# Two decoder layers in one kernel: a new order of the VectorE and ScalarE work in the MLPs' down projections

## Chip, core and metric

The kernel runs on one core of one Trainium2 chip. The metric is the device time of one execution in microseconds (us), as the median of several runs; a lower time is better.

## What is computed

The reference is two layers of a decoder trunk over 1024 tokens and a model width of 1024. Each layer has a mixer (sparse attention with a gated recurrence in layer 0, a gated recurrence with windowed attention in layer 1), an output projection, and a squared-ReLU MLP with 4096 hidden units. The change touches the two MLPs alone:

```python
for layer in range(DEPTH):
    h = rms_norm(x, norm_mix_g[layer])
    ...
    x = x + mix
    h = rms_norm(x, norm_mlp_g[layer])
    x = x + jnp.square(jax.nn.relu(h @ mlp_w_up[layer])) @ mlp_w_down[layer]
```

## The kernel before

Every float32 matrix product is made of three matmuls. An operand is split in a rounded high part (`w_hi`, `uo_hi`, `h_hi`) and the rest (`w_lo`, `uo_lo`, `h_lo`), and the products high by high, low by high and high by low are added up in PSUM. ScalarE makes the high parts, by a copy that rounds. The low part of a weight is a subtraction on GpSimd (`low`, line 936, POOL in the profile), the low part of an activation one on VectorE (`low`, line 2592, DVE).

An MLP runs over eight groups of 512 hidden units. The first is done directly. The others, and the down projection of the first seven, go by a scheme that takes seven products of half-size blocks in place of eight, at the price of sums and differences of the operands. A middle group (`group(i)`, i from 1 to 6) has on TensorE seven up products P0 to P6 and seven down products e0 to e6, each of 24 matmuls of 512 columns. The first group has, behind its up part, a short stretch of matmuls that forms sums of `h` (`combinations`), and then its own e0 to e6. The last group has P0 to P6 and then a plain down projection by four weight units (`down_last`).

The activations of a group are four quarters `quarter(r, c)`. The down products read seven operands made from them: e0 reads quarter (1,1); e1 the difference `s3` (`uo_sum`); e2 the difference `ub` = (1,1) - s3; e3 quarter (0,0); e4 quarter (0,1); e5 quarter (1,0) after (1,1) has been added to it (line 2629); e6 the difference of (0,1) and `ub` (line 2612). Three pairs of buffers `uo_hi`, `uo_lo` hold the operands in turn (`S_OPERAND`), so that the operand of e3 can be written once e1 has been done, that of e4 once e0 has, and so on. TensorE waits ahead of e0 to e6 for 1, 2, 3, 5, 5, 6 and 7 low parts (`LOW_COUNT`) and for one more weight each time.

The down weights of a group are three sums `d1`, `d0`, `d2`, made on GpSimd (line 943) out of four raw blocks, and the four raw blocks. The products of e0 to e6 are left in four pairs of PSUM banks in turn (`S_BANKS`), and VectorE adds them to `x` and `shared` (line 2609). A product may only begin when VectorE has read the pair of banks that it takes.

All engines run their own instructions in the order in which they are written, with semaphores between them. Nothing reorders: a wait holds all that is written behind it. On ScalarE a group ends with `late_operands`, which copies the operands of e3 to e6 and the last two down weights; the first weight of the next group (`UP_SLOTS[0]`) stands behind it. GpSimd's next group begins with the low part of that weight. The raw blocks are loaded by SyncE, each as soon as GpSimd has used the one before in its buffer.

## Time and profile before

| | |
|---|---|
| median of 3 runs | 2649.71 us (2647.24 to 2653.09) |
| profiled execution, own time | 2644.74 us |
| its span | 2643.0 us |
| TensorE (PE) busy | 2380.4 us, 90% |
| GpSimd (POOL) busy | 1422.0 us, 54% |
| VectorE (DVE) busy | 1763.9 us, 67% |
| ScalarE (ACT) busy | 1142.0 us, 43% |

The span is that of one profiled execution. A row of the timeline gives start and duration of one or more instructions of a kind in a row on one engine, and in brackets how long the engine was idle before and what released it. The MLP of layer 0 lies at about 780 to 1520 us, that of layer 1 at about 1905 to the end.

### The profile page before, as it was taken

To read this page: it belongs to the slowest core of one execution; us is meant where nothing else is said; L and a number is where in the kernel's file an instruction comes from. 1 tells how busy PE (TensorE), PEld (TensorE's weight loads), DVE (VectorE), ACT (ScalarE), POOL (GpSimd) and SP (SyncE) were. 2 spreads that over 40 slices of the span, in tenths; PEclk is the share of its full clock that TensorE was granted. 3 is DMA by queue.
4 is the path that set the end of the run, shared out by engine and by line. 5 is a ranking of instruction groups with operands and counts; after the bars stand their busy time and mean duration, and the time that the engine had idled before them with its cause. 6 is when DMAs were issued, how large, how long until landed. Compare 5 with 4: busy or idle time off the path is not lost.

```text
span 2643.0 us, 31005 instructions
## 1 busy us (share of the span) xinstructions
PE 2380.4 (90%) x10811; PEld 1916.8 (73%) x10833; DVE 1763.9 (67%) x2390; ACT 1142.0 (43%) x1867; POOL 1422.0 (54%) x719
## 2 busy tenths in 40 slices
PE   8899997889899988898889999889998888988998
PEld 6678874558887766686668777767876667766777
DVE  7879879889854576457647557666555764575473
ACT  4556887676554233323332455354532333233320
POOL 3203427998724665766577222255145657565762
PEclk9999998999999999999999999989999999999999
DMA  5311130022013432433244222221034233423342
GB/s 158 90 38 51 49 100 5 17 59 78 9 49 127 144 118 75 148 135 110 80 150 133 84 84 56 72 78 32 24 143 144 82 109 135 146 84 111 133 137 80
DMA packets 167356, 241.57 MB, mean 91 GB/s; under 512 B 27529, under 2 KB 110546, under 8 KB 167250
## 3 DMA queue, kind: packets, MB, share of 16 engines
q1 hardware_dynamic: 160786, 233.65, 27.2%
q10 hardware_dynamic: 6464, 6.56, 0.8%
q8 instruction: 60, 0.98, 0.2%
q14 instruction: 46, 0.38, 0.0%
HBM read 204.25 MB, written 26.21 MB: 87 GB/s over the span
## 4 chain that ended last, share of the span: by engine, by line
PE 28%; POOL 26%; issue 23%; DVE 11%; ACT 6%; DMA 5%; SPq 1%; POOLq 0%; ACTq 0%; another core or an unknown queue 0%; DVEq 0%
POOL w_lo L936 13%; PE ps L2805 7%; PE ps L2806 7%; PE ps L2807 7%; DMA w_raw<-in_mlp_w_down 4%; POOL w_sum L943 4%; POOL w_raw L943 3%; ACT signs L1669 3%; POOL PL L1146 2%; POOL cl L1188 1%; POOL w_lo L923 1%; PE ps L2798 1%; POOL w_hi L917 1%; DVE ps L2363 1%; DVE ps L2261 1%
## 5 line engine op out<-in xcount | busy, mean ns | idle before, releaser
L936 POOL TENSOR_TENSOR w_lo<-w_raw,w_hi 128x1024 fp32r<-128x1024 f32 x148 | 384.6, 2615 | 346.5 <-ACT w_hi L1478 309.3
L2805 PE MATMUL ps<-w_hi,uo_hi 128*128 128x512 f32 x784 | 320.5, 409 | 145.4 <-DVE uo_lo L2592 140.2
L923 POOL TENSOR_TENSOR w_lo<-w_raw,w_hi 128x1024 fp32r<-128x1024 f32 x61 | 159.4, 2613 | 353.4 <-ACT w_hi L1692 349.6
L2806 PE MATMUL ps<-w_lo,uo_hi 128*128 128x512 f32 x784 | 315.5, 402 | 0.0
L2807 PE MATMUL ps<-w_hi,uo_lo 128*128 128x512 f32 x784 | 315.0, 402 | 0.0
L2805 PE MATMUL ps<-h_hi,w_hi 128*128 128x512 f32 x776 | 311.5, 401 | 0.0
L2807 PE MATMUL ps<-h_hi,w_lo 128*128 128x512 f32 x776 | 303.8, 392 | 0.0
L2806 PE MATMUL ps<-h_lo,w_hi 128*128 128x512 f32 x776 | 303.6, 391 | 0.0
L2609 DVE TENSOR_TENSOR x_res<-ps,x_res 128x1024 f32<-128x1024 f32 x224 | 265.1, 1216 | 46.5 <-PE ps L2807 40.3
L2805 PEld LDWEIGHTS ps<-w_hi,uo_hi 128*128 128x128 f32 x784 | 154.4, 197 | 190.1 <-issue 152.4
L1478 ACT ACTIVATE w_hi<-w_raw 128x1024 fp32r<-128x1024 f32 x143 | 148.9, 1053 | 252.6 <-PE ps L2807 188.4
L2807 PEld LDWEIGHTS ps<-w_hi,uo_lo 128*128 128x128 f32 x784 | 153.4, 196 | 33.7
L2806 PEld LDWEIGHTS ps<-w_lo,uo_hi 128*128 128x128 f32 x784 | 154.5, 197 | 31.6
L2979 PE MATMUL ps<-h_hi,w_hi 128*128 128x512 f32 x448 | 174.3, 389 | 0.0
L2980 PE MATMUL ps<-h_lo,w_hi 128*128 128x512 f32 x448 | 174.3, 389 | 0.0
L2981 PE MATMUL ps<-h_hi,w_lo 128*128 128x512 f32 x448 | 174.3, 389 | 0.0
L2807 PEld LDWEIGHTS ps<-h_hi,w_lo 128*128 128x128 f32 x776 | 146.3, 189 | 31.6
L2806 PEld LDWEIGHTS ps<-h_lo,w_hi 128*128 128x128 f32 x776 | 146.6, 189 | 30.0 <-issue 1.9
L2805 PEld LDWEIGHTS ps<-h_hi,w_hi 128*128 128x128 f32 x776 | 146.4, 189 | 30.4 <-issue 2.4
L936 POOL TENSOR_TENSOR w_lo<-w_sum,w_hi 128x1024 fp32r<-128x1024 f32 x56 | 156.5, 2815 | 11.6 <-ACT w_hi L1478 7.6
L2673 DVE TENSOR_TENSOR ps<-ps,ub 128x1024 f32<-128x1024 f32 x14 | 17.3, 1233 | 203.9 <-ACT ps L1590 203.9
L1478 ACT ACTIVATE w_hi<-w_sum 128x1024 fp32r<-128x1024 f32 x56 | 57.9, 1058 | 201.2 <-POOL w_sum L943 201.2
(436 smaller groups left out, 5882.5 us busy)
## 6 DMA issues: line engine op xcount, KB each, us to landing
uo_hi<-scr_h SPq DMA_DIRECT2D x82, 512.0 KB, 3.9
uo_lo<-scr_h SPq DMA_DIRECT2D x82, 512.0 KB, 4.8
w_raw<-in_mlp_w_up SPq DMA_DIRECT2D x64, 512.0 KB, 3.6
w_raw<-in_mlp_w_down SPq DMA_DIRECT2D x64, 512.0 KB, 5.2
w_raw<-in_even_w_in SPq DMA_DIRECT2D x23, 512.0 KB, 3.9
x_res<-in_x SPq DMA_DIRECT2D x16, 512.0 KB, 7.8
t<-xg SPq DMA_DIRECT2D x120, 64.0 KB, 2.0
scr_h<-h_hi SPq DMA_DIRECT2D x12, 512.0 KB, 7.6
```

What stands on the lines that cost most here:

```text
L923: g.tensor_tensor(w_lo[:, k, :], w_raw[:, n % 2, :], w_hi[:, k, :].bitcast(F32), ALU.subtract).then_inc(w_ready, 1)
L936: g.tensor_tensor(w_lo[:, slot, :], source, w_hi[:, slot, :].bitcast(F32), ALU.subtract) \
L943: g.tensor_tensor(out_, in0, in1, op).then_inc(sums_ready, 1)
L1478: s.activation(w_hi[:, slot, :], source, ACT.Copy).then_inc(w_hi_ready, 1)
L1669: s.activation(signs[:, 0:w], keys, ACT.Sign, bias=tkc[:, q - 2:q - 1], accum_out=cnt[:, q - 2:q - 1]).then_inc(level_counted, 1)
L2609: ins = v.tensor_tensor(dst, ps[:, bank:bank + 2, :], dst, ALU.add)
L2805: t_.matmul(out_, ah, bh, start=first, stop=False)
L2806: t_.matmul(out_, ah, bl, start=False, stop=False)
L2807: return t_.matmul(out_, al, bh, start=False, stop=last)
L2979: t_.matmul(out_, ah, bh, start=begins and k == 0, stop=False, skip_group_check=not begins)
L2980: t_.matmul(out_, ah, bl, start=False, stop=False, skip_group_check=not begins)
L2981: ins = t_.matmul(out_, al, bh, start=False, stop=k == 3, skip_group_check=not begins)
```

## The change

VectorE in a middle group: the sum that completes quarter (1,0) (`mixed`) goes from ahead of the down products' additions to behind those of e2. The rest of `s3` goes ahead of the squaring of quarter (0,1). The difference for e6 (`last_sum`) and the low parts for e3 to e6 get new places among the additions (`downs`). The first group keeps its old order under the name `first_downs`.

ScalarE in a middle group: operand e0 is copied ahead of the weight sum for e0; the relu of quarter (1,0) goes ahead of the other two weight sums; two raw weights go behind the copies for e1 and e2. In `late_operands` the copies for e3 and e4 and the last two weights change places, and the copy for e5 now waits for `mixed`.

TensorE in the first group waits for the sums of `h` bank by bank and no longer for all of them. In the last group ScalarE rounds the four last weight units (`last_unit`), which GpSimd did before (`split_high`); two of these units take other slots (`LAST_SLOTS`).

```diff
-        LAST_SLOTS = (2, 3, 4, 5)
+        LAST_SLOTS = (2, 5, 3, 4)
...
                 for n in range(n0 + MLP_UNITS - 4, n0 + MLP_UNITS):
-                    split_unit(n)
+                    split_low(n)
...
                 def late_operands(i, slots):
 
+                    sums_at(i, 0)
+                    operand(4, quarter(0, 1))
                     act.wait_ge(raw_landed[2], 32 * i + (l0[2] + 32))
-                    sums_at(i, 0)
+                    if slots is not FIRST_SLOTS:
+                        weights(slots[5], raws[2])
+                    sums_at(i, 1)
+                    operand(3, quarter(0, 0))
                     if slots is FIRST_SLOTS:
                         sums_at(i, 2)
-                    weights(slots[5], raws[2])
-                    operand(4, quarter(0, 1))
+                        weights(slots[5], raws[2])
                     act.wait_ge(raw_landed[3], 32 * i + (l0[3] + 32))
-                    sums_at(i, 1)
                     weights(slots[6], raws[3])
-                    operand(3, quarter(0, 0))
+                    act.wait_ge(u_squared, 4 * i + (q0 + 3))
                     sums_at(i, 2)
                     operand(5, quarter(1, 0))
                     act.wait_ge(u_squared, 4 * i + (q0 + 4))
...
+                def last_unit(j):
+                    n = n0 + MLP_UNITS - 4 + j
+                    act.wait_ge(raw_landed[n % 2], landed[n])
+                    for used in last_uses(n):
+                        act.wait_ge(*used)
+                    s.activation(w_hi[:, slot_of(n), :], w_raw[:, n % 2, :], ACT.Copy).then_inc(w_hi_ready, 1)
...
+                    add_sums(i, 0, 0)
+                    add_sums(i, 0, 2)
+                    add_sums(i, 1, 0)
+                    low(i, 4, 4, quarter(0, 1))
+                    low(i, 5, 3, quarter(0, 0))
+                    add_sums(i, 1, 2)
+                    add_sums(i, 2, 0)
+                    add_sums(i, 2, 2)
+                    mixed()
+                    last_sum()
+                    add_sums(i, 3, 0)
+                    low(i, 6, 5, quarter(1, 0))
+                    add_sums(i, 3, 2)
+                    summed(i, 4)
+                    low(i, 7, 6, ub[:])
+                    for e in range(4, 7):
+                        add_sums(i, e, 0)
+                        add_sums(i, e, 2)
...
+                            if slots is FIRST_SLOTS and d in (0, 3) and t % 2 == 0:
+                                pe.wait_ge(quarters_done, first_rests(layer) + (14 if d == 0 else 16))
...
-                    pe.wait_ge(quarters_done, first_rests(layer) + 16)
```

The first place is VectorE's order in a middle group, from the squaring of quarter (1,0) to e0's additions. Before:

```order
1001 L2662 TENSOR_TENSOR u_all<-ps,u_all 128x2x512
1003 L2625 TENSOR_TENSOR uo_sum<-u_all 128x1024
1006 L2662 TENSOR_TENSOR u_all<-ps,u_all 128x2x512
1007 L2628 TENSOR_TENSOR ub<-u_all,uo_sum 128x1024
1008 L2629 TENSOR_TENSOR u_all<-u_all 128x2x512
1011 L2592 TENSOR_TENSOR uo_lo_64<-uo_sum,uo_hi_61 128x1024
1013 L2592 TENSOR_TENSOR uo_lo_65<-ub,uo_hi_62 128x1024
1016 L2609 TENSOR_TENSOR x_res<-ps,x_res 128x2x512
```

And now:

```order
1001 L2705 TENSOR_TENSOR u_all<-ps,u_all 128x2x512
1003 L2670 TENSOR_TENSOR uo_sum<-u_all 128x1024
1005 L2672 TENSOR_TENSOR ub<-u_all,uo_sum 128x1024
1008 L2608 TENSOR_TENSOR uo_lo_64<-uo_sum,uo_hi_61 128x1024
1010 L2705 TENSOR_TENSOR u_all<-ps,u_all 128x2x512
1012 L2608 TENSOR_TENSOR uo_lo_65<-ub,uo_hi_62 128x1024
1015 L2624 TENSOR_TENSOR x_res<-ps,x_res 128x2x512
```

`uo_lo_64` is the low part for e1. It stood behind a squaring (line 2662), `ub` and the sum of quarter (1,0); now only `ub` stands between it and `s3`.

The second place is VectorE among the additions of the down products, now, where `uo_lo_63`, `uo_lo_64` and `uo_lo_65` are the low parts for e4, e3 and e5:

```order
1019 L2624 TENSOR_TENSOR x_res<-ps,x_res 128x2x512 x2
1021 L2608 TENSOR_TENSOR uo_lo_63<-u_all,uo_hi_60 128x1024
1023 L2608 TENSOR_TENSOR uo_lo_64<-u_all,uo_hi_61 128x1024
1025 L2624 TENSOR_TENSOR x_res<-ps,x_res 128x2x512 x2
1027 L2624 TENSOR_TENSOR shared<-ps,shared 128x1024
1029 L2624 TENSOR_TENSOR shared<-ps,shared 128x1024
1030 L2631 TENSOR_TENSOR u_all<-u_all 128x2x512
1031 L2628 TENSOR_TENSOR ub<-u_all,ub 128x1024
1033 L2624 TENSOR_TENSOR shared<-ps,shared 128x1024
1034 L2624 TENSOR_TENSOR x_res<-ps,x_res 128x2x512
1036 L2608 TENSOR_TENSOR uo_lo_65<-u_all,uo_hi_62 128x1024
```

The sum of quarter (1,0) and the difference for e6 now stand in the middle of the additions, ahead of those of e3.

The third place is ScalarE in a middle group, from the relu of quarter (0,0) on. Before:

```order
731 L1566 ACTIVATE u_all<-ps 128x2x512
733 L1478 ACTIVATE w_hi<-w_sum 128x1024
735 L1481 ACTIVATE uo_hi_60<-u_all 128x1024
737 L1478 ACTIVATE w_hi<-w_sum 128x1024 x2
739 L1566 ACTIVATE u_all<-ps 128x2x512
741 L1478 ACTIVATE w_hi<-w_raw 128x1024
743 L1481 ACTIVATE uo_hi_61<-uo_sum 128x1024
```

And now:

```order
731 L1576 ACTIVATE u_all<-ps 128x2x512
733 L1481 ACTIVATE uo_hi_60<-u_all 128x1024
735 L1478 ACTIVATE w_hi<-w_sum 128x1024
737 L1576 ACTIVATE u_all<-ps 128x2x512
739 L1478 ACTIVATE w_hi<-w_sum 128x1024 x2
741 L1481 ACTIVATE uo_hi_61<-uo_sum 128x1024
```

The relu of quarter (1,0) (the second `u_all<-ps`) now comes ahead of the two weight copies, and e0's operand ahead of the first of the three.

## Rows read from the trace of the kernel before

**Rows 1.** The page, head and part 1.

```profile
span 2643.0 us, 31005 instructions
...
PE 2380.4 (90%) x10811; PEld 1916.8 (73%) x10833; DVE 1763.9 (67%) x2390; ACT 1142.0 (43%) x1867; POOL 1422.0 (54%) x719
```

**Rows 2.** Waits of PE: who, for whom, us in all, times, longest.

```profile
PE ps L2805 <- DVE uo_lo L2592: 140.2, 14, 10.4
```

**Rows 3.** Timeline of PE, layer 0: first matmuls behind the MLP's long waits.

```profile
838.16 0.50 PE L2805 MATMUL ps<-w_hi,uo_hi 128*128 128x512 f32 x1 [1.66 <-DVE h_lo L2649]
...
865.23 0.77 PE L2805 MATMUL ps<-w_hi,uo_hi 128*128 128x512 f32 x1 [10.45 <-DVE uo_lo L2592]
...
942.45 0.79 PE L2805 MATMUL ps<-w_hi,uo_hi 128*128 128x512 f32 x1 [9.94 <-DVE uo_lo L2592]
...
1119.59 0.79 PE L2805 MATMUL ps<-w_hi,uo_hi 128*128 128x512 f32 x1 [9.94 <-DVE uo_lo L2592]
...
1386.01 0.79 PE L2805 MATMUL ps<-w_hi,uo_hi 128*128 128x512 f32 x1 [9.96 <-DVE uo_lo L2592]
...
1462.75 0.80 PE L2805 MATMUL ps<-w_hi,u_hi 128*128 128x512 f32 x1 [3.65 <-POOL w_lo L923]
```

**Rows 4.** Timeline of PE around the start of one group's e0.

```profile
1103.33 0.39 PE L2979 MATMUL ps<-h_hi,w_hi 128*128 128x512 f32 x1
...
1104.01 0.40 PE L2805 MATMUL ps<-w_hi,uo_hi 128*128 128x512 f32 x1
```

**Rows 5.** Stretches: us, busy us of PE, PEld, DVE, ACT, POOL, PE's clock, DMA.

```profile
1463.00:1468.00 5.00, 5.00 (x12) 3.88 (x13) 2.63 (x1) 0.00 (x0) 4.92 (x3) 0.50 0.36 105
838.10:840.10 2.00, 1.94 (x8) 1.61 (x9) 0.00 (x1) 0.93 (x1) 1.94 (x1) 1.00 0.00 0
```

**Rows 6.** Timeline of DVE ahead of e1 in one middle group.

```profile
1100.15 1.38 DVE L2592 TENSOR_TENSOR uo_lo<-u_all,uo_hi 128x1024 fp32r<-128x1024 f32 x1 [4.33 <-ACT uo_hi L1481]
...
1104.69 2.54 DVE L2625 TENSOR_TENSOR uo_sum<-u_all 128x1024 f32<-128x1024 f32 x1
...
1112.81 3.37 DVE L2629 TENSOR_TENSOR u_all<-u_all 128x1024 f32<-128x1024 f32 x1
1116.30 3.15 DVE L2592 TENSOR_TENSOR uo_lo<-uo_sum,uo_hi 128x1024 fp32r<-128x1024 f32 x1
1119.38 1.21 DVE L2592 TENSOR_TENSOR uo_lo<-ub,uo_hi 128x1024 fp32r<-128x1024 f32 x1
```

**Rows 7.** Timeline of POOL in the same stretch.

```profile
1098.03 2.42 POOL L943 TENSOR_TENSOR w_sum<-w_sum,w_raw 128x1024 f32<-128x1024 f32 x1
1100.60 8.90 POOL L936 TENSOR_TENSOR w_lo<-w_sum,w_hi 128x1024 fp32r<-128x1024 f32 x3 [0.16 <-POOL w_sum L943]
1109.45 8.92 POOL L936 TENSOR_TENSOR w_lo<-w_raw,w_hi 128x1024 fp32r<-128x1024 f32 x3
```

**Rows 8.** Timeline of ACT in the same stretch: the relu of quarter (1,0).

```profile
1102.39 1.01 ACT L1566 ACTIVATE u_all<-ps 128x1024 f32<-128x1024 f32 x1
```

**Rows 9.** Timelines of ACT, POOL and DVE around the end of e3.

```profile
1049.80 1.06 ACT L1481 ACTIVATE uo_hi<-ub 128x1024 fp32r<-128x1024 f32 x1 [4.38 <-PE ps L2807]
...
1051.88 2.39 POOL L936 TENSOR_TENSOR w_lo<-w_raw,w_hi 128x1024 fp32r<-128x1024 f32 x1 [9.42 <-ACT w_hi L1478]
...
1052.07 3.28 DVE L2592 TENSOR_TENSOR uo_lo<-ub,uo_hi 128x1024 fp32r<-128x1024 f32 x1
```

**Rows 10.** Timeline of DVE: four additions of down products in a row.

```profile
1036.65 4.62 DVE L2609 TENSOR_TENSOR x_res<-ps,x_res 128x1024 f32<-128x1024 f32 x4
```

**Rows 11.** Timeline of POOL between the up and the down weights.

```profile
1083.41 2.41 POOL L943 TENSOR_TENSOR w_raw<-w_raw,w_raw 128x1024 f32<-128x1024 f32 x1 [6.34 <-DMA w_raw<-in_mlp_w_down]
```

**Rows 12.** Timeline of ACT in the first group, behind e2.

```profile
854.90 1.06 ACT L1478 ACTIVATE w_hi<-w_raw 128x1024 fp32r<-128x1024 f32 x1 [15.88 <-PE ps L2807]
```

**Rows 13.** Timeline of POOL ahead of the last down projection: rounding, then rest.

```profile
1457.51 1.90 POOL L917 TENSOR_TENSOR w_hi<-w_raw,onec 128x1024 fp32r<-128x1024 f32 x1
1459.49 3.21 POOL L923 TENSOR_TENSOR w_lo<-w_raw,w_hi 128x1024 fp32r<-128x1024 f32 x1
```

More of the change, by code:

```diff
@@ L2622, in operands, with add_sums @@
-                def operands(i, n):
-                    if n == 0:
-                        v.tensor_tensor(s3, quarter(0, 0), quarter(1, 0), ALU.subtract).then_inc(u_squared, 1)
-                        summed(i, 1)
-                    if n == 1:
-                        v.tensor_tensor(ub[:], quarter(1, 1), s3, ALU.subtract).then_inc(u_squared, 1)
-                        v.tensor_tensor(quarter(1, 0), quarter(1, 0), quarter(1, 1), ALU.add).then_inc(u_squared, 1)
-                        summed(i, 3)
+                def add_sums(i, e, t):
+                    k = S_ORDER[e]
+                    dve.wait_ge(down_done, S_SUMS * i + (g0 + 4 * e + t + 2))
+                    earlier = [n for n in range(e) if set(S_TARGETS[S_ORDER[n]]) & set(S_TARGETS[k])]
+                    if earlier:
+                        dve.wait_ge(x_added, S_SUMS * i + (g0 + 4 * earlier[-1] + t + 2))
+                    for c in S_TARGETS[k]:
+                        dst = shared[:, t:t + 2, :] if c is None else                             x[:, 4 * (1 - c[0]) + t:4 * (1 - c[0]) + t + 2, c[1] * HT:(c[1] + 1) * HT]
+                        bank = S_BANKS[2 * e + t // 2]
+                        ins = v.tensor_tensor(dst, ps[:, bank:bank + 2, :], dst, ALU.add)
+                    ins.then_inc(x_added, 2)
@@ new lines, in last_sum, with mixed, first_downs @@
+                def last_sum():
+                    v.tensor_tensor(ub[:], quarter(0, 1), ub[:], ALU.subtract).then_inc(u_squared, 1)
+                def mixed():
+                    v.tensor_tensor(quarter(1, 0), quarter(1, 0), quarter(1, 1), ALU.add).then_inc(u_squared, 1)
+                def first_downs():
+                    for e in range(7):
+                        add_sums(0, e, 0)
+                        add_sums(0, e, 2)
+                        if e == 0:
+                            last_sum()
+                            low(0, 4, 4, quarter(0, 1))
+                        if e == 1:
+                            low(0, 5, 3, quarter(0, 0))
+                        if e == 2:
+                            low(0, 6, 5, quarter(1, 0))
+                        if e == 3:
+                            summed(0, 4)
+                            low(0, 7, 6, ub[:])
@@ L2632, in first_group, with operands @@
+                def operands(i):
+                    v.tensor_tensor(s3, quarter(0, 0), quarter(1, 0), ALU.subtract).then_inc(u_squared, 1)
+                    summed(i, 1)
+                    v.tensor_tensor(ub[:], quarter(1, 1), s3, ALU.subtract).then_inc(u_squared, 1)
+                    summed(i, 2)
                 def first_group():
@@ L2641, in first_group @@
                             dve.wait_ge(proj_free, h0 + 6)
-                            operands(0, 0)
-                            operands(0, 1)
+                            operands(0)
+                            mixed()
                             low(0, 2, 1, s3)
@@ L2686, in group @@
                         dve.wait_ge(quarters_done, quarters + C12_DONE)
-                        operands(i, 0)
+                        operands(i)
+                        low(i, 2, 1, s3)
                     last_low(3, 1, 0)
@@ L2692, in group @@
                         return
-                    operands(i, 1)
-                    low(i, 2, 1, s3)
                     low(i, 3, 2, ub[:])
```

48 lines of the change are left out of this document (17 added, 31 removed).

## The prediction, made before the run

> **What bounds the kernel now.** The page says that TensorE is busy for 90% of the span and VectorE for 67% [rows 1]. A busy share says nothing of single waits, so the waits of TensorE come next: one line alone makes 140.2 us of them in 14 waits, and it waits for a low part of VectorE [rows 2]. The timeline of TensorE shows where: in each MLP once in the first group (10.45 us) and once in each of six middle groups (9.94 us, each ahead of e1) [rows 3]. The period from one such wait to the next is (1386.01 - 942.45) / 5 = 88.7 us.
>
> A wait costs more than its length. Three matmuls take 1104.01 - 1103.33 = 0.68 us at full clock [rows 4], 0.227 us each and 5.44 us for a product of 24. Behind the wait of 3.65 us, 12 matmuls fill 5.0 us at a granted clock of 0.50, which is the lower level of 1.2 GHz; behind the wait of 1.66 us the clock stays at 1.00 [rows 3, 5]. The middle group has 14 products, 76.2 us. Of the 88.7 us, 12.5 are left: 9.94 us of wait, about 2.3 us of halved clock, and 0.2 us of small change.
>
> What does VectorE do before e1? Four operations between SBUF operands stand in line: `s3`, `ub`, the sum of quarter (1,0), the low part for e1. The first, third and fourth take 2.54, 3.37 and 3.15 us, while the next one of the same kind, with GpSimd idle, takes 1.21 [rows 6]. GpSimd's low parts take 2.4 us alone, but three of them take 8.90 and again 8.92 us [rows 7]. Laid side by side, each starts when the other ends: VectorE's sum of 1104.69 ends at 1107.23, one operation behind the end of GpSimd's second low part. I read it as: these operations take turns, 2.4 us for GpSimd, 1.2 for VectorE. The Trainium skill (SBUF — State Buffer, SBUF: two separate sides) says that the two engines share a pair of ports as an exclusive lock, which whoever starts first holds for the whole instruction, VectorE only with two SBUF inputs. The durations agree. Were they merely long and GpSimd not held, the delays of GpSimd below would drop out, and the sum would be that of the first rival.
>
> **The change, part by part.** I count from E, the end of a group's e3; in the group shown it is 1049.65 (ScalarE is released at 1049.80 [rows 9]). From there TensorE has e4 to e6 and P0 to P6, ten products, 54.4 us, and e0 does start at 1104.01 [rows 4]. GpSimd's chain to the weight for e0 also begins at E, with the first weight of the next group at E + 2.2 [rows 9]; it contains a 6.3 us wait for blocks from memory [rows 11], and its low part for e0 ends about 3.2 us behind 1100.60, at E + 54.1 [rows 7]. So today e0 starts with hardly 0.3 us in hand. Whatever slows GpSimd's chain stops e0.
>
> *Ahead of e0.* e0's operand no longer stands behind a weight that waited for GpSimd. VectorE is idle for 4.33 us before that operand's low part at 1100.15 [rows 6], so quarter (1,1) was done at 1095.8; with a copy of 1.06 us the low part can be asked for at 1097.0. It then falls ahead of GpSimd's sum `d0`, which began at 1098.03 [rows 7], and pushes it back by 1.15 us, to an end at 1101.6. The relu of quarter (1,0) began at 1102.39 [rows 8]; its product P5 ends 5.44 us before e0 starts, at 1098.6, and only one weight copy is now ahead of it, so it begins at 1099.1. With 1.0 us for it and 1.2 for the squaring `s3` is asked for at 1101.4, just before `d0` ends. If it takes its turn there, GpSimd's low part for e0 ends 1.2 us later than today, and e0 starts at E + 55.5 in place of 54.4. TensorE loses 1.2 us.
>
> *Ahead of e1.* `s3` ends at E + 53, GpSimd's low part for e0 at 55.3, `ub` at 56.5, the next low part at 58.8, and the low part for e1 at 59.9. e1 is wanted at 55.5 + 5.4 = 60.9. The wait of 9.94 us and its 2.3 us of low clock go. The squaring of quarter (0,1) and the low part for e2 end within 2.5 us of e1's start; e1's second half and e2 need them after 2.7 and 5.4.
>
> *Among the additions*, from T, e1's start. An addition costs 4.62 / 4 = 1.15 us [rows 10]. Low part for e2 to T + 2.5, four additions to 7.0, low part for e4 to 8.3, then GpSimd's turn to 10.7, low part for e3 to 11.8. e3 is wanted at T + 10.9, so it waits about 1.05 us; E is T + 17.4. VectorE ends the additions of e2 at T + 16.3, `mixed` at 17.5 and the difference for e6 at 18.6. ScalarE, which stood free at E, now waits for `mixed` with the copy for e5, and behind it are queued the copy for e6 and the first weight of the next group; GpSimd waits for that. It begins at E + 3.4 in place of 2.2. The low part for e5 meets it, which it did not before, and the one for e6 also does, as before (3.28 us [rows 9]). GpSimd is 2.4 us late in all. The wait of 6.3 us for memory [rows 11] gives back between none and all of that, as the blocks asked for later have fewer transfers ahead; I take 0.8, nearer to none, because an unhindered load cannot land before it is asked for. VectorE is late too, and e6's second half waits 1.5 us for the bank that e5's additions free; if GpSimd had its turn before the low part for e5, e5 waits 1.65 and e6 2.2 us.
>
> *Sum of a middle group that follows a middle group.* GpSimd's chain is 54.1 + 1.6 (late start and meetings, less the memory's gift), and 1.2 to 2.4 more ahead of e0, where the turns fall worse once it is late: e0 at about E + 57.3, e1 at E + 62.8; if `s3` loses its turn, E + 64.4. With 17.4 the period is 80.2 to 81.8. I take 81.0, so 7.7 us saved, five times in each MLP: 38.5.
>
> *The first group.* TensorE starts its e0 when 14 of 16 sums are read, 1.2 us sooner. ScalarE's copies for e4 and e3 stood behind a weight that waited for the end of e2 (15.88 us idle, then released by TensorE [rows 12]); they now follow e0 and e1. Counted from the start of e0, VectorE comes behind its end (5.6) to one addition, the difference for e6, e4's low part, four additions and e3's low part: 5.6 + 1.15 + 1.2 + 1.2 + 4.6 + 1.2 = 15.0. e2 ends at 16.3. So the 10.45 us wait goes, with 1.6 us of low clock: 13.3 us. Its order on VectorE is the old one, so the next group only loses the 1.2 us at e0: its wait of 9.94 and 0.2 less 1.2 makes 9.2.
>
> *The last group.* From T of group 6 to the last down projection it is 1462.75 - 1386.01 = 76.7 us; now 17.4 + 1.5 + 54.4 + 0.5 = 73.8, 2.9 less. ScalarE's rounding takes four operations of 1.9 us off GpSimd, whose last low part ended at 1462.70 [rows 13]; the four come behind each other's loads, and the last is then ready at about the end of P6, 1459. What is left (0.5) is the low part for the third quarter. Without the 3.65 us wait the clock does not fall: 5.0 us [rows 5] for 12 matmuls in place of 2.7, and a few more, 2.6 us. Together 5.5. Bounds: nothing is gained if the weights are as late as now (0), 6.3 if all goes.
>
> *Moved at no cost:* two raw weights on ScalarE come 4 us later, but GpSimd takes them only when its three other low parts are done; the slots are mere places.
>
> Sum for an MLP 13.3 + 9.2 + 38.5 + 5.5 = 66.5, for both 133 us. The profiled execution took 2644.7 us, which gives 2512; it lies 5.0 us (0.2%) below the median of 2649.7, which gives 2517. I say 2515.
>
> **The rivals.**
> *All is hidden (17%).* VectorE's and GpSimd's turns fall well, or VectorE is early enough. With no stall left, 14 waits of 12.4 us, twice 1.2 and twice 6.3 give 189 us, 2461; with 2.2 us left in each period 161, 2489. For it: GpSimd has idle stretches of nearly 10 us [rows 9]. Against: they lie ahead of its chain, and in the chain there is 0.3 us in hand.
> *Short waits drop the clock (27%).* My waits of 1.4 to 2.9 us lie between 1.66 us, which left the clock at 1.00, and 3.65, which halved it [rows 3, 5]. One drop in each of twelve groups costs 12 x 2.4 = 29 us (2545), two 58 (2573). The Trainium skill (TensorE: Matmul & The Clock Gate, Part 1) says that the clock is halved by how busy the array has been and not by single waits, and that the moment varies; by it some of these would be charged.
> *ScalarE's new wait makes it slower (2%).* Each us by which `mixed` ends behind E delays everything on GpSimd by one. It decides against the change from 11 us on, with `mixed` at E + 12: some 10 additions late. Twelve groups at 13 us late would give 2660. VectorE would have to lose three times what I count.
> *No change (2%).* GpSimd's chain grows until the period is 88.7 again. It would need 7.7 us more meetings, six per group; I count two or three new ones.
>
> **How the numbers follow.** My case, 2490 to 2535, has 50%; all hidden 17, clock 27, neither 2 and 2, and 2 for more than 2590. The range 2476 to 2562 leaves out part of the first rival and the two-drop end of the second. A measurement here tells 0.2% (5 us) from nothing: faster by more 0.96, within 0.02, slower 0.02.
>
> **What would show it.** In the waits of TensorE the 140.2 us line should fall below 30 us in 14 or more short waits; e1's wait should be gone. Waits for GpSimd's weight ahead of e0 should be 1 to 3 us, for VectorE's low part ahead of e3 about 1 us, for additions ahead of e6's second half 1 to 2 us. The period should be 80 to 82 us. The first weight of a group should start on GpSimd 3.4 us behind E. I am wrong if e1 still waits over 2 us, or if the clock is halved in most groups.

## The result and the profile after

The changed kernel takes 2511.16 us (median of 4 runs, 2503.55 to 2514.51), the kernel before, timed beside it, 2649.45 us. The ratio is 0.9473 [0.9448, 0.9498], 138 us less; the forecast was 2515 us. The profiled execution took 2513.01 us, 131.7 less than that of before; by this pair, on which the sum was made, the forecast was 133.

The page of the changed kernel, head and part 1 (against [rows 1]):

```profile
span 2510.3 us, 31037 instructions
...
PE 2362.6 (94%) x10833; PEld 1901.0 (76%) x10833; DVE 1742.0 (69%) x2390; ACT 1151.5 (46%) x1875; POOL 1444.4 (58%) x711
```

The engines do the same work, but for eight roundings of weights that went from GpSimd to ScalarE. VectorE is busy for 22 us less, as fewer of its operations stretch beside GpSimd. GpSimd is busy for 22 us more in spite of the eight: more of its own now stretch beside VectorE. TensorE is busy for 18 us less, as fewer matmuls run at half clock. The waits of TensorE (who, for whom, us in all, times, longest), the rows of the MLPs (against [rows 2]):

```profile
PE ps L2847 <- POOL w_lo L936: 14.6, 12, 1.8
...
PE ps L2847 <- DVE x_res L2624: 9.8, 10, 1.0
...
PE ps L3022 <- DMA uo_lo<-scr_h: 7.1, 9, 1.7
PE ps L2847 <- DVE uo_lo L2608: 6.4, 12, 2.0
```

One line of 140.2 us in 14 waits has become four kinds of short waits, 37.9 us in 43. The third kind is for a streamed piece: a part of the split `h` that SyncE loads back from memory (`scr_h`) during a group, for the up products. The timeline of TensorE shows where the waits stand (against [rows 3]): e0 of the first group and of three middle groups, the other waits of the one at 1159.11 (e3, e6's second half), the longest e1, and the last down projection of layer 0.

```profile
839.16 0.47 PE L2847 MATMUL ps<-w_hi,uo_hi 128*128 128x512 f32 x1 [0.55 <-DVE h_lo L2692]
...
1004.74 0.49 PE L2847 MATMUL ps<-w_hi,uo_hi 128*128 128x512 f32 x1 [2.05 <-DVE uo_lo L2608]
...
1078.39 0.49 PE L2847 MATMUL ps<-w_hi,uo_hi 128*128 128x512 f32 x1 [0.99 <-POOL w_lo L936]
...
1159.11 0.49 PE L2847 MATMUL ps<-w_hi,uo_hi 128*128 128x512 f32 x1 [1.65 <-POOL w_lo L936]
...
1175.96 0.49 PE L2847 MATMUL ps<-w_hi,uo_hi 128*128 128x512 f32 x1 [0.24 <-DVE uo_lo L2608]
...
1196.27 0.50 PE L2847 MATMUL ps<-w_hi,uo_hi 128*128 128x512 f32 x1 [0.99 <-DVE x_res L2624]
...
1239.89 0.49 PE L2847 MATMUL ps<-w_hi,uo_hi 128*128 128x512 f32 x1 [1.79 <-POOL w_lo L936]
...
1402.16 0.77 PE L2847 MATMUL ps<-w_hi,u_hi 128*128 128x512 f32 x1 [2.76 <-issue]
```

From one e0 to the next it is 1159.11 - 1078.39 = 80.7 and 1239.89 - 1159.11 = 80.8 us. In the group at 1159 nothing waits ahead of e1. In two of the twelve middle groups e1 still waits, 2.05 us at 1004.74 and 2.01 us at 1987.54. The stretch from the first e0 to the last down projection was 1462.75 - 838.16 = 624.6 us in layer 0 and is 563.0 now; in layer 1 it went from 626.7 to 561.6.

VectorE from `ub` on in that group (against [rows 6]; the row at 1171.22 holds the low parts for e4 and e3, the one at 1180.28 is `mixed`):

```profile
1156.79 3.28 DVE L2672 TENSOR_TENSOR ub<-u_all,uo_sum 128x1024 f32<-128x1024 f32 x1
1160.19 3.24 DVE L2608 TENSOR_TENSOR uo_lo<-uo_sum,uo_hi 128x1024 fp32r<-128x1024 f32 x1
...
1171.22 4.61 DVE L2608 TENSOR_TENSOR uo_lo<-u_all,uo_hi 128x1024 fp32r<-128x1024 f32 x2
...
1180.28 1.21 DVE L2631 TENSOR_TENSOR u_all<-u_all 128x1024 f32<-128x1024 f32 x1
```

`s3` took 1.22 us there, at 1155.53, just ahead of GpSimd's low part for e0 (1155.75). In the group whose e1 waits at 1004.74 GpSimd's came first, and `s3` ends a turn later; VectorE's and GpSimd's timelines:

```profile
995.22 2.71 DVE L2670 TENSOR_TENSOR uo_sum<-u_all 128x1024 f32<-128x1024 f32 x1
```

```profile
994.44 9.09 POOL L936 TENSOR_TENSOR w_lo<-w_sum,w_hi 128x1024 fp32r<-128x1024 f32 x3 [0.16 <-POOL w_sum L943]
```

ScalarE and GpSimd behind the end of e3, which is 1175.96 + 5.44 = 1181.4 (against [rows 9]): operand e5 comes behind `mixed`, then e6's, then the first weight, and GpSimd takes it at 1184.8.

```profile
1181.60 1.06 ACT L1481 ACTIVATE uo_hi<-u_all 128x1024 fp32r<-128x1024 f32 x1 [9.27 <-DVE u_all L2631]
1182.73 1.06 ACT L1481 ACTIVATE uo_hi<-ub 128x1024 fp32r<-128x1024 f32 x1
1183.70 1.04 ACT L1478 ACTIVATE w_hi<-w_raw 128x1024 fp32r<-128x1024 f32 x1
```

```profile
1184.82 3.46 POOL L936 TENSOR_TENSOR w_lo<-w_raw,w_hi 128x1024 fp32r<-128x1024 f32 x1 [6.72 <-ACT w_hi L1478]
```

### The profile page after: what moved, and what is told of

Same layout as the page of the kernel before. It is cut to its first block, busy times and chain, and to the rows that moved or that the text cites. A ratio compares the mean times of both kernels' runs of the same rounds, so it can differ in the third digit from the quotient of the medians.

```text
span 2510.3 us, 31037 instructions
## 1 busy us (share of the span) xinstructions
PE 2362.6 (94%) x10833; PEld 1901.0 (76%) x10833; DVE 1742.0 (69%) x2390; ACT 1151.5 (46%) x1875; POOL 1444.4 (58%) x711
## 4 chain that ended last, share of the span: by engine, by line
PE 34%; POOL 22%; issue 17%; DVE 13%; DMA 6%; ACT 6%; SPq 1%; POOLq 0%; ACTq 0%; DVEq 0%
POOL w_lo L936 11%; PE ps L2847 8%; PE ps L2849 8%; PE ps L2848 8%; DMA w_raw<-in_mlp_w_down 5%; POOL w_sum L943 4%; ACT signs L1685 3%; POOL w_raw L943 2%; POOL PL L1146 2%; POOL cl L1188 1%; PE ps L2840 1%; PE ps L3022 1%; PE ps L3024 1%; PE ps L3023 1%; DVE ps L2379 1%
## 5 line engine op out<-in xcount | busy, mean ns | idle before, releaser
L936 POOL TENSOR_TENSOR w_lo<-w_raw,w_hi 128x1024 fp32r<-128x1024 f32 x148 | 407.9, 2775 | 169.9 <-ACT w_hi L1478 132.6
L923 POOL TENSOR_TENSOR w_lo<-w_raw,w_hi 128x1024 fp32r<-128x1024 f32 x61 | 154.4, 2533 | 368.5 <-ACT w_hi L1708 349.9
L2847 PE MATMUL ps<-w_hi,uo_hi 128*128 128x512 f32 x784 | 310.8, 396 | 31.9 <-POOL w_lo L936 14.6
L2848 PE MATMUL ps<-w_lo,uo_hi 128*128 128x512 f32 x784 | 306.9, 391 | 0.0
L2849 PE MATMUL ps<-w_hi,uo_lo 128*128 128x512 f32 x784 | 306.9, 391 | 0.0
L2847 PEld LDWEIGHTS ps<-w_hi,uo_hi 128*128 128x128 f32 x784 | 147.9, 189 | 77.2 <-issue 33.0
L1481 ACT ACTIVATE uo_hi<-u_all 128x1024 fp32r<-128x1024 f32 x56 | 59.5, 1062 | 282.9 <-DVE u_all L2631 105.4
L936 POOL TENSOR_TENSOR w_lo<-w_sum,w_hi 128x1024 fp32r<-128x1024 f32 x56 | 167.3, 3006 | 12.4 <-ACT w_hi L1478 7.7
L2849 PEld LDWEIGHTS ps<-w_hi,uo_lo 128*128 128x128 f32 x784 | 148.0, 189 | 31.4
L2848 PEld LDWEIGHTS ps<-w_lo,uo_hi 128*128 128x128 f32 x784 | 148.1, 189 | 29.6
```

The lines of the kernel that those rows point to most:

```text
L923: g.tensor_tensor(w_lo[:, k, :], w_raw[:, n % 2, :], w_hi[:, k, :].bitcast(F32), ALU.subtract).then_inc(w_ready, 1)
L936: g.tensor_tensor(w_lo[:, slot, :], source, w_hi[:, slot, :].bitcast(F32), ALU.subtract) \
L2847: t_.matmul(out_, ah, bh, start=first, stop=False)
L2848: t_.matmul(out_, ah, bl, start=False, stop=False)
L2849: return t_.matmul(out_, al, bh, start=False, stop=last)
```

## Experiments

All start from the changed kernel. Ratios are to the kernel before, timed beside each on the same chip, where it took 2645.6 to 2649.8 us. "Less" is the difference of these two medians; the text compares kernels by it. The intervals of the ratios make a difference between two of these kernels uncertain by 5 to 8 us. "Period" is the mean of five from e0 to e0 in layer 0, from the starts of e0 in each trace.

| kernel | us | less, us | ratio | period, us |
|---|---|---|---|---|
| before | 2649.45 | 0 | 1 | 88.7 |
| changed | 2511.16 | 138.3 | 0.9473 [0.9448, 0.9498] | 80.9 |
| undo_first | 2544.21 | 105.6 | 0.9599 [0.9584, 0.9615] | 80.6 |
| undo_last | 2524.67 | 125.1 | 0.9524 [0.9503, 0.9544] | 80.6 |
| act_old | 2540.44 | 109.3 | 0.9599 [0.9581, 0.9617] | 83.0 |
| mixed_back | 2532.91 | 116.9 | 0.9563 [0.9544, 0.9581] | 81.9 |
| rest_behind | 2511.64 | 134.0 | 0.9487 [0.9474, 0.95] | 80.7 |
| stream_first | 2543.74 | 101.9 | 0.9619 [0.9606, 0.9631] | 83.3 |
| up0_early | 2508.0 | 137.6 | 0.9486 [0.9472, 0.95] | 79.6 |
| up0_mid | 2499.08 | 147.7 | 0.9439 [0.9424, 0.9454] | 79.6 |
| s5_behind | 2486.21 | 159.4 | 0.9395 [0.9381, 0.9408] | 78.8 |
| up6_first | 2491.52 | 154.8 | 0.9415 [0.9401, 0.9429] | 79.3 |
| s5_up6 | 2468.55 | 177.7 | 0.9326 [0.9314, 0.9339] | 77.3 |
| s5_up6_up0 | 2483.24 | 163.0 | 0.9388 [0.9375, 0.94] | 78.1 |

### One part undone at a time

**undo_first** gives the first group its old order and its old wait for all 16 sums.

```diff
+                    if slots is FIRST_SLOTS:
+                        act.wait_ge(raw_landed[2], l0[2] + 32)
+                        sums_at(i, 0)
+                        sums_at(i, 2)
+                        weights(slots[5], raws[2])
+                        operand(4, quarter(0, 1))
...
-                            if slots is FIRST_SLOTS and d in (0, 3) and t % 2 == 0:
-                                pe.wait_ge(quarters_done, first_rests(layer) + (14 if d == 0 else 16))
...
+                    pe.wait_ge(quarters_done, first_rests(layer) + 16)
```

> The changed kernel with the first group as it was before: ScalarE's old order of the last copies there, and TensorE waits for all 16 sums of h. My theory: the wait of about 10.5 us ahead of e3 with its low clock and 1 us ahead of e0 come back once in each MLP, and since the next group is counted from the end of e3, nothing makes it up: 13.3 us per MLP, about 2537 us in place of 2511. Rival: GpSimd uses the wait to get ahead, and the following groups give most of it back: under 10 us in all, at most 2521.

33 us slower. The old wait is back to the digit, and the clock behind it is halved; TensorE's timeline and the stretch behind it (us, busy us of PE, PEld, DVE, ACT, POOL, PE's clock, DMA) in this kernel:

```profile
869.36 0.77 PE L2863 MATMUL ps<-w_hi,uo_hi 128*128 128x512 f32 x1 [10.45 <-DVE uo_lo L2624]
```

```profile
869.00:874.00 5.00, 4.64 (x11) 3.71 (x12) 3.66 (x4) 0.00 (x0) 0.00 (x0) 0.50 0.01 3
```

From the first e0 to the next it takes 91.35 us in place of 77.28 (layer 1: 91.93 in place of 78.71), 27.3 us for both layers, and e0 itself waits 1.66 in place of 0.55 us, 2.2 for both. That is 29.5 of the 33. The forecast's 13.3 per layer was small by about 1.4. The rival, under 10 us in all, is out.

**undo_last** lets GpSimd round the last four units again, in the old slots.

```diff
-        LAST_SLOTS = (2, 5, 3, 4)
+        LAST_SLOTS = (2, 3, 4, 5)
...
-                    split_low(n)
+                    split_unit(n)
...
```

> The changed kernel with the last four weight units rounded by GpSimd again, in the old slots. My sum had 5.5 us per MLP for this part (2522); the changed kernel's trace still shows waits of 2.8 and 0.9 us there, so 3 to 5 us per MLP are likelier: 2517 to 2521. Rival: the last low part of the third quarter sets the start of the last down projection, whoever rounds: under 2 us in all.

13 us slower, where 6 to 10 were expected: the last down projections wait for GpSimd's low part again, 9.1 us in two waits. TensorE's waits and timeline in this kernel:

```profile
PE ps L2841 <- POOL w_lo L923: 9.1, 2, 4.6
```

```profile
1402.37 0.50 PE L2841 MATMUL ps<-w_hi,u_hi 128*128 128x512 f32 x1 [4.62 <-POOL w_lo L923]
```

The changed kernel has 2.76 and 0.93 us at these places, so 5.4 us are waits alone; 11 were forecast for both layers with the clock. The profiled executions of the two kernels lie only 5.7 us apart (2518.66 and 2513.01), so these traces do not show where the rest of the 13 us is.

In the changed kernel the row names no releaser ("issue"), but the low part of the third quarter (`u_lo`) ends just ahead of the start in both layers, at 1402.06 for 1402.16 and at 2462.61 for 2462.72. In layer 0 it came late because an operation before it, which took 1.22 us in layer 1, stood through a turn of GpSimd's; VectorE's and GpSimd's timelines:

```profile
1392.17 3.41 DVE L2722 SCALAR_TENSOR_TENSOR u_new<-u_new 128x1024 f32<-128x1024 f32 x1
...
1400.19 1.87 DVE L2711 TENSOR_TENSOR u_lo<-u_new,u_hi 128x1024 fp32r<-128x1024 f32 x1 [1.12 <-ACT u_hi L1618]
```

```profile
1392.11 2.38 POOL L923 TENSOR_TENSOR w_lo<-w_raw,w_hi 128x1024 fp32r<-128x1024 f32 x1 [2.19 <-ACT w_hi L1562]
```

**act_old** puts ScalarE's middle groups back to the old order up to the copy for e2.

```diff
+                    act.wait_ge(sums_ready, sums + 7)
+                    weights(S_SLOTS[0], fp32(S_SLOTS[0]))
...
-                    act.wait_ge(sums_ready, sums + 7)
-                    weights(S_SLOTS[0], fp32(S_SLOTS[0]))
-                    product_done(6)
-                    positive(BANK_Y, 1, 0)
...
+                    product_done(6)
+                    positive(BANK_Y, 1, 0)
+                    act.wait_ge(raw_landed[0], 32 * i + (l0[0] + 32))
+                    weights(S_SLOTS[3], raws[0])
...
```

> The changed kernel with ScalarE's old order in the middle groups up to the copy for e2: weight sum ahead of e0's operand, both weight sums and the raw weight ahead of the relu of quarter (1,0). My theory: s3 starts 3 us later and with it e1's low part, so e1 waits 2 to 3 us in each of twelve groups, while the wait ahead of e0 shrinks by about 1.2: plus 20 to 45 us, 2531 to 2556. Rival: only GpSimd's chain sets the period, and this order delays nothing on it: no change or up to 10 us faster.

29 us slower. In the middle groups e0 hardly waits (0.5 us in one), and e1 waits in all twelve, 4.3 us each, where 2 to 3 were expected. TensorE's waits, VectorE ahead of e0, TensorE's e1 and the stretch behind it:

```profile
PE ps L2847 <- DVE uo_lo L2608: 52.1, 12, 4.4
```

```profile
1159.16 1.38 DVE L2608 TENSOR_TENSOR uo_lo<-u_all,uo_hi 128x1024 fp32r<-128x1024 f32 x1 [4.33 <-ACT uo_hi L1481]
```

```profile
1173.01 0.79 PE L2847 MATMUL ps<-w_hi,uo_hi 128*128 128x512 f32 x1 [4.34 <-DVE uo_lo L2608]
```

```profile
1173.00:1178.00 5.00, 4.99 (x12) 3.98 (x13) 5.00 (x4) 2.01 (x2) 3.90 (x2) 0.50 0.63 195
```

VectorE's idle 4.33 us ahead of e0's low part are those of [rows 6]. So ScalarE's early copy and relu are what costs TensorE its 0.25 to 1.79 us at e0, and they save 4.3 us of wait and the clock at e1.

**mixed_back** puts the sum of quarter (1,0) back ahead of e1's low part.

```diff
-                    mixed()
...
+                        mixed()
```

> The changed kernel with the sum of quarter (1,0) put back ahead of e1's low part. My theory: one more turn against GpSimd, 1.2 to 3.4 us, of which 1.1 fit before e1: e1 waits up to 2.5 us, while ScalarE no longer waits for that sum behind e3 and GpSimd's chain begins 1.2 us earlier, which takes as much off the wait ahead of e0. Net 0 to 1.5 us per group: 2511 to 2530. Rival (this move is where the whole 10 us came from): plus 3 to 4 us and a clock drop per group, over 2560.

21 us slower, 2 more than the upper end of what was expected. In the profiled execution 5.1 us lie ahead of the first MLP, where it came later to its first e0 (844.3 in place of 839.2; the traces of all these kernels spread from 834.7 to 844.3), and 17.8 between the first e0 and the last down projection of the two layers. The relief that was expected at e0, 1.2 us a group, hardly came: its waits are 12.6 us in 11 here and 14.6 in 12 in the changed kernel. VectorE has one more turn to wait for, and e1 waits for it:

```profile
1166.84 3.32 DVE L2631 TENSOR_TENSOR u_all<-u_all 128x1024 f32<-128x1024 f32 x1
```

```profile
1173.60 0.49 PE L2847 MATMUL ps<-w_hi,uo_hi 128*128 128x512 f32 x1 [2.04 <-DVE uo_lo L2608]
```

**rest_behind** puts e1's low part back behind the squaring of quarter (0,1).

```diff
-                        low(i, 2, 1, s3)
...
+                    low(i, 2, 1, s3)
```

> The changed kernel with e1's low part put back behind the squaring of quarter (0,1). In the changed kernel's trace that low part stands for 2 us waiting for GpSimd's turn to end, and the squaring (1.2 us, which takes no turn) fits into that time. My theory of turns: no change, within 4 us. Rival (operations are long by themselves and simply add up): e1 comes 1.2 us later less 1.1 of slack in some groups and shifts what follows, plus 8 to 14 us.

No change that the timing can tell (one execution of 4719 us stands apart from the others at 2507 to 2512, and the ratio leaves it out). The squaring falls into a turn of GpSimd's that the low part would have waited for: in this kernel's trace the squaring at 1162.44 takes 1.22 us and the low part behind it 2.07, where the changed kernel's took 3.24. So this part of the new order is worth nothing by itself.

One at a time, these edits raise the period by 2.1 us (act_old), 1.0 (mixed_back) and nothing (rest_behind), while the whole change took 7.8 us off it. The parts are worth more together than singly, and no run undoes them together. Nor does any run undo the new places of the low parts for e3 to e6 among the additions, or the new order in `late_operands` of the middle groups: what these two are worth is not shown.

### Which path ends at e0

The forecast counted GpSimd's chain from the end of e3 and gave e0's wait to its late start. Four edits ask whether that is so.

**stream_first** loads the fifth piece of streamed activations, for which TensorE waits 0.5 to 1.7 us in the changed kernel, ahead of the fourth block of down weights.

```diff
-                    for r, n in ((1, 5), (0, 6), (2, 6), (3, 7)):
+                    for r, n in ((1, 5), (0, 6), (2, 6)):
...
+                    sp.wait_ge(w_ready, before + 7)
+                    load_down(i, 3)
```

> The changed kernel with the last streamed piece of h issued ahead of the load of the fourth down block. In the changed kernel TensorE waits for that piece 0.4 to 1.7 us in most middle groups, about 10 us in all, which I had not forecast. My theory: GpSimd's chain sets the period, so these waits go and those ahead of e0 grow by as much or more, as the fourth block now lands later: 2508 to 2520. Rival: waits of TensorE add up, minus 8 to 12 us, 2500.

36 us slower, which neither side had. The waits for the piece are gone, but the block is asked for only at 1150.63 (SyncE) and GpSimd's first sum of it starts at 1156.32, after a wait of 6.36 us (4.13 in the changed kernel). e0 and e1 pay, in TensorE's waits:

```profile
1150.63 0.39 SPq L792 DMA_DIRECT2D w_raw<-in_mlp_w_down  x1
```

```profile
1156.32 3.44 POOL L945 TENSOR_TENSOR w_sum<-w_raw,w_raw 128x1024 f32<-128x1024 f32 x1 [6.36 <-DMA w_raw<-in_mlp_w_down]
```

```profile
PE ps L2849 <- POOL w_lo L938: 29.4, 12, 3.0
PE ps L2849 <- DVE uo_lo L2610: 18.7, 17, 2.0
```

**up0_early** rounds the first up weight right behind the end of e3, ahead of ScalarE's wait for `mixed`.

```diff
+                    act.wait_ge(raw_landed[0], 32 * i + (l0[0] + 48))
+                    sums_at(i, 3)
+                    weights(UP_SLOTS[0], raws[0])
...
-                    act.wait_ge(raw_landed[0], 32 * i + (l0[0] + 16))
-                    sums_at(i - 1, 3)
-                    weights(UP_SLOTS[0], raws[0])
```

> The changed kernel with the first up weight of the next group rounded right behind the end of e3, ahead of the copies for e5 and e6. GpSimd's chain then begins 2.1 us earlier after the end of e3. My theory: the chain sets the period, the waits ahead of e0 (14.6 us in 12) nearly vanish: 12 to 22 us faster, 2489 to 2499. Rival: the landing of the down blocks sets the chain, and what is won at its start is waited away there: under 5 us.

No gain that the timing can tell (0.9486 against 0.9473, the intervals overlap), where 12 to 22 us were expected. This looked like a refutation, and the first reading of it was that the chain is caught again behind its start, as GpSimd's timeline shows:

```profile
1130.19 2.40 POOL L936 TENSOR_TENSOR w_lo<-w_raw,w_hi 128x1024 fp32r<-128x1024 f32 x1 [0.64 <-ACT w_hi L1478]
1140.04 2.41 POOL L943 TENSOR_TENSOR w_raw<-w_raw,w_raw 128x1024 f32<-128x1024 f32 x1 [7.45 <-DMA w_raw<-in_mlp_w_down]
```

The sixth up weight stands on ScalarE behind a copy of P0's product, which TensorE releases at 1128.14; GpSimd waits for that weight, and then for blocks. But the period had fallen by 1.3 us, and what rose was the stretch from the first e0 to the second, from 77.3 to 83.0 us (layer 1: 78.7 to 84.0). There the weight waits for the end of e3, and e5's copy, which in the first group does not have to wait for `mixed`, now stands behind it. VectorE then idles for 6.24 us ahead of e5's low part, and TensorE waits 1.69 us ahead of e5 and 1.80 in e6. ScalarE's timeline, first group of up0_early; in the changed kernel the copy for e5 begins at 857.72:

```profile
861.70 1.06 ACT L1478 ACTIVATE w_hi<-w_raw 128x1024 fp32r<-128x1024 f32 x1 [3.49 <-PE ps L2849]
862.66 1.04 ACT L1481 ACTIVATE uo_hi<-u_all 128x1024 fp32r<-128x1024 f32 x1
```

**up0_mid** makes the edit in the middle groups alone.

```diff
+                    if slots is not FIRST_SLOTS:
+                        act.wait_ge(raw_landed[0], 32 * i + (l0[0] + 48))
+                        sums_at(i, 3)
+                        weights(UP_SLOTS[0], raws[0])
...
```

> The first up weight is rounded right behind the end of e3 in the middle groups alone; in the first group it stays behind the copy for e6. With the edit in all groups the five periods after the first fell from 80.9 to 79.6 us, while the stretch from the first e0 to the second rose from 77.3 to 83.0 us in layer 0 and from 78.7 to 84.0 in layer 1, where ScalarE's copy for e5 had stood ready at 857.7 and came at 862.7 behind the weight. Theory: the lost 11 us were the first group's alone, and the middle groups do gain from a chain that starts sooner: first stretch 77 to 78 us, later periods 79.6, time 2495 to 2501 us, e0's waits about 1.0 us. Rival: GpSimd's chain is caught again at P0 and P2 and at the blocks from memory, and the shorter periods only made up for time lost in the first group: periods back at 80.5 to 81, time 2507 to 2513 us.

The theory holds, and not the rival: 2499.08 us, 9 less than the changed kernel (close to what the timing can tell), the first stretch 78.3 us and the periods 79.6 in layer 0. In layer 1 the mean period is 80.4 (80.8 in the changed kernel), because one group there took 83.1 us behind a wait of 2.03 us at e1; the other four took 79.4 to 80.1. So it was the experiment up0_early that was badly set, in the first group, and not the path that was wrong. e3 starts at 1093.32 in the group whose first weight GpSimd's timeline shows, and ends 5.44 us later:

```profile
1100.22 2.41 POOL L936 TENSOR_TENSOR w_lo<-w_raw,w_hi 128x1024 fp32r<-128x1024 f32 x1 [4.77 <-ACT w_hi L1478]
```

The chain starts at E + 1.5 in place of E + 3.4, and up to 1.3 of the 1.9 us reach TensorE. They show less at e0 than in the waits for a streamed piece, and e6 takes some back; TensorE's waits in this kernel:

```profile
PE ps L2852 <- DVE x_res L2629: 15.8, 12, 1.3
...
PE ps L3027 <- DMA uo_lo<-scr_h: 1.9, 2, 1.6
```

**up6_first** rounds the last up weight ahead of a copy in PSUM (both stand behind the end of P2), and takes its low part ahead of the sum that waits for memory.

```diff
+                    low(before + 7, UP_SLOTS[6], raws[3])
...
-                    low(before + 7, UP_SLOTS[6], raws[3])
...
+                    act.wait_ge(raw_landed[3], 32 * i + (l0[3] + 16))
+                    weights(UP_SLOTS[6], raws[3])
...
-                    act.wait_ge(raw_landed[3], 32 * i + (l0[3] + 16))
-                    weights(UP_SLOTS[6], raws[3])
```

(Between the last two places stand the wait for VectorE's additions and the copy.)

> The changed kernel, but the last up weight of a middle group is rounded ahead of ScalarE's PSUM copy, and its low part stands on GpSimd ahead of the sum that waits for the down blocks. The run with an early first weight gained nothing, so my first theory (GpSimd's chain counts from the end of e3) fell. New theory: the chain to e0's weight is tied to TensorE's P0 and P2: down blocks that land behind the streamed pieces, then the low part of the last up weight, then the load of the fourth block (3.7 us), then three sums. With that low part 2.4 us sooner the fourth block lands 2.4 us sooner, the waits ahead of e0 (15 us in 12) and those for the streamed piece behind that load (7 us) go: 12 to 22 us faster, 2489 to 2499. Rival: turns against VectorE ahead of e0 eat it, under 5 us.

As expected: 16 us faster, and the waits at e0 and for the streamed piece are gone. GpSimd now waits for a weight first and hardly for memory, since the fourth block is asked for sooner; its waits of 7.26 and 4.13 us for blocks in the changed kernel have become one of 5.74 for the weight and one of 1.71 for a block:

```profile
1137.42 2.40 POOL L936 TENSOR_TENSOR w_lo<-w_raw,w_hi 128x1024 fp32r<-128x1024 f32 x1 [5.74 <-ACT w_hi L1478]
...
1143.88 2.39 POOL L943 TENSOR_TENSOR w_sum<-w_raw,w_raw 128x1024 f32<-128x1024 f32 x1 [1.71 <-DMA w_raw<-in_mlp_w_down]
```

TensorE's waits in this kernel; what is left stands at e3 and at e6's second half:

```profile
PE ps L2847 <- DVE uo_lo L2608: 14.8, 12, 1.2
...
PE ps L2847 <- DVE x_res L2624: 11.6, 12, 1.0
```

### The turn ahead of e3

**s5_behind** holds GpSimd's sixth low part of down weights until VectorE has made the low part for e3.

```diff
+                        if r == 2 and i is not None:
+                            pool.wait_ge(u_ready, 7 * i + (u0 + 5))
...
```

> The changed kernel with GpSimd's sixth low part of the down weights held back until VectorE has made the low part for e3. If the two take turns, VectorE's low parts for e4 and e3 take 1.2 us each in place of 1.3 and 3.4, and e3 no longer waits (0.4 us each): 2 to 6 us faster. If that low part is long for another reason it stays at 3.4 us, and nothing changes.

21 us faster, where 2 to 6 were expected. The mechanism is the one expected, and what it reaches was not: only e3's own wait had been counted. VectorE's two low parts for e4 and e3 take 2.41 us in place of 4.61, and GpSimd pays 2.38 us of idle time that nobody waits for:

```profile
1167.87 2.41 DVE L2610 TENSOR_TENSOR uo_lo<-u_all,uo_hi 128x1024 fp32r<-128x1024 f32 x2
```

```profile
1170.44 4.76 POOL L936 TENSOR_TENSOR w_lo<-w_raw,w_hi 128x1024 fp32r<-128x1024 f32 x2 [2.38 <-DVE uo_lo L2610]
```

VectorE is 2.2 us earlier from there to the group's end, so the waits at e3 and at e6's second half go together, and the period falls by 2.1. The Trainium skill (SBUF — State Buffer, SBUF: two separate sides) says that of two such operations the second is blocked in full until the first ends, and does not run slower beside it. The trace agrees: 4.61 less 2.41 us is 2.2 us, close to one whole GpSimd operation of 2.4. (The prediction's "only with two SBUF inputs" is narrower than that section of the Trainium skill, which names VectorE's two-port modes beside them; no run here shows one.)

**s5_up6** takes s5_behind and up6_first together.

> Both together: GpSimd's sixth down low part held back until e3's low part is made, and the last up weight first. The two work on different waits (ahead of e3 and e6; ahead of e0), so they should add up: 22 us and 12 to 20, 2469 to 2477. If instead one wait only took the other's place, no more than the better of the two, 2486.

The two gains add up: 2468.55 us, 39 less than the changed kernel (the single ones 21 and 16), 6.7% below the kernel before. In the MLPs' groups one kind of wait is left over 2 us in all:

```profile
PE ps L2849 <- DVE x_res L2626: 7.0, 12, 0.6
```

**s5_up6_up0** adds up0_early to it.

> The kernel with both, and the first up weight rounded right behind the end of e3 as well. By the new theory GpSimd's chain is tied to P0 and P2 and not to the end of e3, so nothing more is gained: within 5 us of the kernel with both. By the old theory up to 2 us in each of twelve groups: 10 to 20 us faster.

15 us slower than s5_up6, which neither theory had. GpSimd's early low part meets VectorE's low part for e5 (1.94 us; 1.21 in s5_up6), e5's additions come later, and e6's second half waits. VectorE's timeline and TensorE's waits in this kernel:

```profile
1097.67 1.94 DVE L2610 TENSOR_TENSOR uo_lo<-u_all,uo_hi 128x1024 fp32r<-128x1024 f32 x1
```

```profile
PE ps L2849 <- DVE x_res L2626: 22.8, 16, 1.8
```

The rest is the first group's, as in up0_early: its stretch takes 81.9 us in place of 76.3, 11 us for both layers. But the periods also rose, from 77.3 to 78.1, where up0_mid's had fallen: once GpSimd's chain has slack, its earlier start buys nothing and costs a meeting.

## Why the prediction was right, and where it was not

**What bounds the kernel: right.** The long waits and the half clock behind them were the cost. They are gone, and undo_first and act_old bring each back.

**Turns of VectorE and GpSimd: right.** `ub` and e1's low part take 3.28 and 3.24 us, and a held-back GpSimd operation removes such a stretch (s5_behind). GpSimd is held too, as the forecast had it: the changed kernel's low parts on it take up to 3.46 us, where 2.39 is their time alone [rows 9].

**e0 late by 1.2 us, later more: right.** The rows say 0.99, 1.65, 1.79; 1.2 was counted for the first and 1.4 once the chain was late. act_old, in which this wait is gone and e1's is back, shows that ScalarE's new order makes it.

**The first weight at E + 3.4: right** (1184.82 - 1181.4 = 3.4). **GpSimd's chain from there to e0: right as a path that holds TensorE, not as the only one.** up0_mid starts it 1.9 us sooner and wins 1.3 a period in layer 0; up6_first leaves its start alone, moves one low part inside it, and e0's waits are gone (period -1.7).

**The memory's gift of 0.8 us: wrong.** Of the wait of 6.3 us for memory [rows 11] the forecast said that it gives back between none and all of a late start, and counted 0.8. It gave nothing back. In the waits of GpSimd (its rows `w_raw` and `w_sum`, for down blocks) the kernel before has 80.9 + 45.1 us and the changed kernel 86.1 + 53.7, and in the group before 1159 the wait is 7.26. A second wait, for the fourth block, of 4.13 us in the kernel before (GpSimd at 1092.30) and in the changed one alike, was not in the forecast at all. What it missed is why these waits are so long: the load of the fourth block stands behind the low part of the last up weight, which stands behind the sum that waits for the third; up6_first turns 7.26 and 4.13 us of such waits into 1.71, behind one of 5.74 for the weight.

**Ahead of e1: right in ten groups of twelve.** The prediction's own sign of being wrong, "if e1 still waits over 2 us", came in two, by 2.05 and 2.01 us. They are its branch "if `s3` loses its turn", priced there at 1.6 us (E + 64.4 less 62.8), and the clock fell behind both.

**Among the additions: right in kind, mis-sized.** By the starts of the matmuls e3 begins 0.39 us late (1175.96 less the 0.23 pitch less 1175.34) where 1.05 was counted, and e6's second half 1.15 us where 1.5 was.

**Not foreseen:** the waits for a streamed piece, 7.1 us in nine. The forecast period of 81.0 us (80.4 to 81.4 measured) was met in part by luck, as its errors offset each other: by starts, in the group from 1159 on, e3 and e6 lost 1.0 us less than counted, e0 0.5 more (1.94 for 1.4) and the piece 0.6 that was not counted. stream_first says that they can't be had by a mere exchange of two loads; s5_up6 has none of them.

**First group:** 13.3 was counted; 14.1 and 13.2, and 1.1 at e0 in each layer, are what its undoing costs. The first stretch became 77.3 us from 88.6. The term for the group behind it has a slip: 9.94 and 0.2 less 1.2 is 8.9 and not 9.2. **Last group:** 11 us for both layers were counted, 13 were lost without it (undo_last). Of the wait there 0.5 us was to be left, by the low part of the third quarter. It is that low part indeed, but it leaves 0.93 us in layer 1 and 2.76 in layer 0, where GpSimd's turn delayed it and the clock fell to 0.67 over the next 5 us.

**The sum:** 66.5 us per layer were forecast to the start of the last down projection and a little behind it; the stretches gave 61.6 and 65.1 us, 126.7 in both. Of the rest of the profiled pair's 132.7 us of span, 4.2 lie between the last down projection of layer 0 and the first e0 of layer 1, where 1.1 is e0's shorter wait, and 2.8 behind the last start of layer 1; the first e0 of layer 0 itself came 1.0 us later. That the higher clock makes the most of the 4.2 and 2.8 is likely, not shown. Layer 0 gained less partly by its longer wait at the end (2.76 for 0.93 us), partly because its stretch was the shorter one before (624.6 for 626.7); the wait of 2 us ahead of e1, with the clock behind it, stands once in each layer.

**The rivals.** "Short waits drop the clock" had 27% and came true in two groups of twelve, for about 1.6 us each and not the 2.4 counted: in the stretches below 15 matmuls stand where 22 do at full clock, 7 x 0.227 us. The Trainium skill (TensorE: Matmul & The Clock Gate, Part 1), which the prediction names there, speaks of how busy the array has been of late, and a long wait alone can lower the clock by it; "not by single waits" says more than the Trainium skill does. "All is hidden" was rightly held for less likely; s5_up6 shows what it needed, one operation held back and one moved, and lies in its range (2461 to 2489). "ScalarE's new wait makes it slower" and "no change" had nothing to them.

## What to carry to other kernels

Where two engines take turns, look at each short operation that stretches by the whole of one of the other's, and hold back the long one that nobody waits for: here a single wait on GpSimd gave 21 us. In a late chain, look inside for a load that stands behind a step that waits for another load, before moving its start; and when an edit shows no gain, compare the stretches one by one, since a gain in the loop and a loss in its first pass had cancelled here. Count the waits that stand behind the one removed; they came to 38 us beside 140.

## What the runs showed of the hardware

The granted clock of TensorE after a wait of about 2 us is not settled by its length. Stretches of 5 us behind the waits of 2.05 us at 1004.74 and of 1.65 us at 1159.11 in the changed kernel (columns as above):

```profile
1004.70:1009.70 5.00, 4.96 (x15) 3.97 (x16) 5.00 (x4) 2.01 (x2) 5.00 (x2) 0.66 0.26 87
...
1159.10:1164.10 5.00, 4.99 (x22) 4.15 (x23) 4.88 (x3) 3.34 (x4) 5.00 (x2) 1.00 0.00 0
```

The 2.04 us wait of mixed_back at 1173.60, of nearly the same length as the first, left it at 1.00; the stretch behind it in that kernel:

```profile
1173.60:1178.60 5.00, 5.00 (x22) 4.16 (x23) 5.00 (x4) 2.01 (x2) 5.00 (x2) 1.00 0.26 86
```

The Trainium skill (TensorE: Matmul & The Clock Gate, Part 1) says that the moment at which the clock rises varies from run to run, by where the first matmul falls. No run here shows what sets it; two waits of one length with two outcomes fit a moment that is not tied to the wait. Nor did a longer wait have to cost more: behind the 4.62 us of undo_last the first matmul ran in 0.50 us, as at full clock, the first slow one came 0.6 us later, and the next 5 us had 15 matmuls at a mean of 0.66, as behind the 2.05 us.
